# Context sums of six decoded sequences as three products of rounded halves, and four weight tiles loaded later

## The reference

```python
def attend_seq(args):
    pt, qn, qr, cn, krn = args
    c_all = jnp.concatenate([cache_ckv[layer, pt].reshape(past, KV_LORA).astype(cn.dtype), cn], axis=0)
    kr_all = jnp.concatenate([cache_krope[layer, pt].reshape(past, QK_ROPE).astype(krn.dtype), krn], axis=0)
    k_nope = rmsnorm(jnp.einsum('lc,chd->lhd', c_all, w_uk), g_kn)
    s = jnp.einsum('qhd,lhd->hql', qn, k_nope) + jnp.einsum('qhr,lr->hql', qr, kr_all)
    p = jax.nn.softmax(jnp.where(mask[None], s.astype(jnp.float32) * SOFTMAX_SCALE, -jnp.inf), axis=-1)
    ctx = jnp.einsum('hql,lc->qhc', p.astype(c_all.dtype), c_all)
    return jnp.einsum('qhc,chd->qhd', ctx, w_uv).reshape(s_new, N_HEADS * V_HEAD)
```

## Time and profile before

| | |
|---|---|
| median of three runs | 1902.29 us (1901.44 to 1902.49) |
| the profiled execution, its own time | 1903.54 us |
| span in the profile | 1901.7 us |
| TensorE busy | 1872.1 us, 98% of the span |
| VectorE, ScalarE, GpSimd busy | 1098.8, 904.0 and 806.1 us |
| TensorE's granted clock | 0.998 of full speed over the span |

### The profile page before, as it was taken

One profiled execution on the slowest core, in us unless ns is written; L12 is line 12 of the kernel. 1 busy time (PEld: TensorE's weight loads), 2 busy tenths in 40 slices (PEclk: granted clock), 3 DMA queues, 4 the chain that ended last, 5 costly groups with the idle time before them and its releaser, 6 DMA issues.

```text
span 1901.7 us, 35322 instructions
## 1 busy us (share of the span) xinstructions
PE 1872.1 (98%) x13021; PEld 1802.9 (95%) x13021; DVE 1098.8 (58%) x1950; ACT 904.0 (48%) x1858; POOL 806.1 (42%) x814
## 2 busy tenths in 40 slices
PE   7999999999999999999999999999999999999998
PEld 7886679999999999999999999999999999999998
DVE  4677756565556555544645644547773564564464
ACT  4456655554555455343424333347754342433333
POOL 3340013432223224253473474385755347347435
PEclk9999999999999999999999999999999999999999
DMA  5320101211111110222333232232222233323223
GB/s 153 67 57 3 26 20 44 80 33 47 35 39 32 48 35 17 71 80 78 89 89 88 78 98 81 79 109 78 75 79 78 78 88 90 88 83 95 77 86 97
DMA packets 253093, 131.63 MB, mean 69 GB/s; under 512 B 43073, under 2 KB 250754, under 8 KB 252882
## 3 DMA queue, kind: packets, MB, share of 16 engines
q1 hardware_dynamic: 252514, 128.56, 24.2%
q10 hardware_dynamic: 444, 1.29, 0.2%
HBM read 126.21 MB, written 3.61 MB: 68 GB/s over the span
## 4 chain that ended last, share of the span: by engine, by line
PE 94%; DVE 3%; ACT 1%; issue 1%; DMA 1%; SPq 0%; POOL 0%; DVEq 0%; ACTq 0%; POOLq 0%
PE ps L208 13%; PE ps L211 13%; PE ps L209 13%; PE ps L1275 7%; PE ps L1273 7%; PE ps L1274 7%; PE ps L1912 5%; PE ps L1910 5%; PE ps L1916 5%; PE ps L1303 3%; PE ps L259 2%; PE ps L251 2%; PE ps L252 2%; PE ps L1049 2%; PE ps L1240 2%; PE ps L265 1%
## 5 line engine op out<-in xcount | busy, mean ns | idle before, releaser
L208 PE MATMUL ps<-split,whi 128*128 128x288 f32 x1840 | 541.6, 296 | 1.4 <-DVE arena L807 1.0
L209 PE MATMUL ps<-split,whi 128*128 128x288 f32 x1840 | 539.0, 294 | 0.0
L211 PE MATMUL ps<-split,wlo 128*128 128x288 f32 x1840 | 526.7, 295 | 0.0
L195 POOL TENSOR_TENSOR wlo<-raw,whi 128x1024 fp32r<-128x1024 f32 x127 | 307.4, 2423 | 377.7 <-ACT whi L172 370.3
L208 PEld LDWEIGHTS ps<-split,whi 128*128 128x128 f32 x1840 | 345.3, 188 | 3.7 <-issue 3.0
L209 PEld LDWEIGHTS ps<-split,whi 128*128 128x128 f32 x1840 | 345.2, 188 | 0.4
L211 PEld LDWEIGHTS ps<-split,wlo 128*128 128x128 f32 x1840 | 339.9, 188 | 0.0
L1273 PE MATMUL ps<-split,split 128*128 128x384 f32 x768 | 268.2, 349 | 0.0
L1523 DVE TENSOR_REDUCE ssq<-arena 128x16 f32<-128x1024 f32 x128 | 156.1, 1220 | 186.6 <-ACT arena L1385 186.6
L1385 ACT ACTIVATE arena<-ps 128x384 f32<-128x384 f32 (+1 forms) x384 | 174.7, 457 | 184.4 <-PE ps L1275 181.4
L1275 PE MATMUL ps<-split,split 128*128 128x384 f32 x768 | 257.9, 336 | 0.0
(11 more groups left out here) (343 smaller groups left out, 3587.3 us busy)
## 6 DMA issues: line engine op xcount, KB each, us to landing
raw<-in_ffn_w_up SPq DMA_DIRECT2D x96, 512.0 KB, 3.7
raw<-in_ffn_w_down SPq DMA_DIRECT2D x48, 512.0 KB, 3.9
arena<-in_cache_ckv SPq DMA_DIRECT2D x128, 128.0 KB, 2.0
raw<-in_rec_w_in SPq DMA_DIRECT2D x16, 512.0 KB, 3.9
raw<-in_attn_w_o SPq DMA_DIRECT2D x8, 512.0 KB, 5.3
raw<-in_rec_w_out SPq DMA_DIRECT2D x8, 512.0 KB, 4.3
raw<-in_attn_w_down SPq DMA_DIRECT2D x7, 512.0 KB, 7.4
raw<-in_attn_w_uq SPq DMA_DIRECT2D x48, 64.0 KB, 2.1
```

The source lines that it names most:

```text
L195: pool.tensor_tensor(wlo[:, t % RING, :], raw[:, t % RING, :], f32(whi[:, t % RING, :]), ALU.subtract).then_inc(w_lo, 1)
L208: pe.matmul(o, wh, a, start=first, stop=False, skip_group_check=resumed)
L209: pe.matmul(o, wh, b, start=False, stop=False, skip_group_check=resumed)
L211: mm = pe.matmul(o, wl, a, start=False, stop=last, skip_group_check=resumed)
```

## The change

In the tails of sequences 0 to 5 the context sum is made like the other products. ScalarE rounds each cached page (258 columns: the 256, a column of ones and a copy of it) into the memory of `raw`/`wlo` in pages 0 to 7 of the next sequence, two pages of rows in each (`rows_high_act`), GpSimd writes the low halves over the cached rows (`rows_low_pool`), ScalarE rounds the probabilities of part c in page 9+c (`probs_high_act`), VectorE makes their low halves in the same page (`probs_low_dve`), and TensorE multiplies three times for each block (`context_halved`). The tails of sequences 6 and 7 stay as they were. Since `raw` is in use until then, SP loads the four output tiles only in the middle of the last sequence's page loads, when the context of sequence 5 is done. Three smaller edits: the columns of ones are two wide, `cnat` with them, and the last step of the maximum touches the 64 rows that hold new keys.

```diff
-        cnat = sb("cnat", [TN, KL + 1])
+        cnat = sb("cnat", [TN, KL + 2])
...
+        HALVED = NB - 2
+        c_rows = wlo[:].rearrange("p a b -> p (a b)")
+        c_last = area(A_P + 7424, 260, dt=F32R)
+        c_new = sb("c_new", [TN, 264], F32R)
+        c_new_lo = area(A_P + 7424 + 776, KL, dt=F32R)
+        cpg_lo = area(A_QC, 2 * PAGES, 260, dt=F32R)
+        s_lo = [area(A_P + i * SEQ_BLOCKS * HQ, SEQ_BLOCKS, HQ, dt=F32R) for i in range(2)]
+        s_hi_of = [area(A_V + 3328, 5, HQ, dt=F32R), area(A_P + 7424 + 264, 4, HQ, dt=F32R)]
+        row_hi, ROW_HI0 = d_ss, 4
+        row_lo, ROW_LO0 = d_rs, 4
+        prob_hi, PROB_HI0 = d_ln, 3
+        prob_lo, PROB_LO0 = d_sq, 7
+
+        def row_high(k):
+            if k == PAGES:
+                return c_new[:, 0:KL + 2]
+            return c_last[:, 0:KL + 2] if k == PAGES - 1 else c_rows[:, 260 * k:260 * k + KL + 2]
+
+        def row_low(par, k):
+            return c_new_lo[0:TN, :] if k == PAGES else cpg_lo[:, par * PAGES + k, 0:KL]
+
+        def rows_high_act(act, b, par, i):
+
+            if i == 0 and b:
+                act.wait_ge(x_ctx, b)
+            if i == 0 and b == 0:
+                act.copy(row_high(PAGES), cnat[:, :]).then_inc(row_hi, 1)
+            for k in (2 * i, 2 * i + 1):
+                act.copy(row_high(k), cpg[:, par * PAGES + k, 0:KL + 2]).then_inc(row_hi, 1)
+
+        def rows_low_pool(pool, b, par, i):
+
+            if i == 0 and b == 0:
+                pool.wait_ge(row_hi, ROW_HI0)
+                pool.tensor_tensor(row_low(par, PAGES), cnat[:, 0:KL], f32(row_high(PAGES))[:, 0:KL], ALU.subtract)\
+                    .then_inc(row_lo, 1)
+            for k in (2 * i, 2 * i + 1):
+                pool.wait_ge(row_hi, ROW_HI0 + PAGES * b + k + 1)
+                pool.tensor_tensor(row_low(par, k), cpg[:, par * PAGES + k, 0:KL], f32(row_high(k))[:, 0:KL],
+                                   ALU.subtract).then_inc(row_lo, 1)
+            pool.wait_ge(row_lo, ROW_LO0 + PAGES * b + 2 * i + 2)
+
+        def probs_high_act(act, b, par, c):
+            act.wait_ge(x_exp, 4 * b + c + 1)
+            act.copy(s_hi_of[c % 2][:, 0:len(PARTS[c]), :], part(s_all[par], c)).then_inc(prob_hi, 1)
+
+        def probs_low_dve(dve, b, par, c):
+            dve.wait_ge(prob_hi, PROB_HI0 + 4 * b + c + 1)
+            ks = PARTS[c]
+            hi = f32(s_hi_of[c % 2])
+            m = min(ks[-1] + 1, PAGES)
+            ins = dve.tensor_tensor(s_lo[par][:, ks[0]:m, :], s_all[par][:, ks[0]:m, :], hi[:, 0:m - ks[0], :], ALU.subtract)
+            if ks[-1] == PAGES:
+                ins = dve.tensor_tensor(s_lo[par][0:TN, PAGES, :], s_all[par][0:TN, PAGES, :], hi[0:TN, m - ks[0], :],
+                                        ALU.subtract)
+            ins.then_inc(prob_lo, 1)
+
+        def context_halved(pe, b, par, c):
+
+            pe.wait_ge(prob_lo, PROB_LO0 + 4 * b + c + 1)
+            pe.wait_ge(row_lo, ROW_LO0 + PAGES * b + min(PARTS[c][-1] + 1, PAGES))
+            for j, k in enumerate(PARTS[c]):
+                n = P if k < PAGES else TN
+                hi, lo = s_hi_of[c % 2][0:n, j, :], s_lo[par][0:n, k, :]
+                pe.matmul(ps[:, 7, 0:KL + 2], hi, row_high(k), start=(k == 0), stop=False)
+                pe.matmul(ps[:, 7, 0:KL], hi, row_low(par, k), start=False, stop=False)
+                mm = pe.matmul(ps[:, 7, 0:KL + 2], lo, row_high(k), start=False, stop=(k == SEQ_BLOCKS - 1))
+            return mm
...
             if 10 <= i <= 13:
                 if i == 10:
                     pe.wait_ge(x_mbs, b + 1)
-                pe.wait_ge(x_exp, 4 * b + i - 9)
-                for k in PARTS[i - 10]:
+                if b < HALVED:
+                    mm = context_halved(pe, b, par, i - 10)
+                else:
+                    pe.wait_ge(x_exp, 4 * b + i - 9)
+                for k in PARTS[i - 10] if b >= HALVED else ():
                     n = P if k < PAGES else TN
-                    rhs = cpg[:, par * PAGES + k, 0:KL + 1] if k < PAGES else cnat[:, :]
+                    rhs = cpg[:, par * PAGES + k, 0:KL + 1] if k < PAGES else cnat[:, 0:KL + 1]
                     mm = pe.matmul(ps[:, 7, 0:KL + 1], s_all[par][0:n, k, :], rhs, start=(k == 0),
                                    stop=(k == SEQ_BLOCKS - 1))
                 if i == 13:
...
+                if tail and b - 1 < HALVED:
+                    if i < PAGES // 2:
+                        rows_high_act(act, b - 1, 1 - par, i)
+                    if 9 <= i <= 12:
+                        probs_high_act(act, b - 1, 1 - par, i - 9)
...
+                if 1 <= n // PAGES <= HALVED and n % PAGES < PAGES // 2:
+                    pool.wait_ge(kr_in, n + 2)
+                    rows_low_pool(pool, n // PAGES - 1, (n // PAGES - 1) % 2, n % PAGES)
...
-                dve.tensor_tensor(mx, mx, s_all[par][:, PAGES, :], ALU.max).then_inc(x_max, 1)
+                dve.tensor_tensor(mx[0:TN, :], mx[0:TN, :], s_all[par][0:TN, PAGES, :], ALU.max).then_inc(x_max, 1)
...
+                    if b - 1 < HALVED and 9 <= i <= 12:
+                        probs_low_dve(dve, b - 1, 1 - par, i - 9)
...
             wo = proj_src("attn_w_o")
-            sp.wait_ge(p_o, NH)
-            for d in range(4):
-                load_tile(sp, WO0 + d, wo(d))
-            with sp.Fori(0, 3) as r:
+            with sp.Fori(0, 2) as r:
                 for par in range(2):
                     for i in range(PAGES):
                         page_load(sp, r * 2 + 2 + par, par, i, True)
+            for b in (LAST - 1, LAST):
+                for i in range(PAGES):
+                    page_load(sp, b, b % 2, i, True)
+                    if b == LAST and i == 3:
+                        sp.wait_ge(x_ctx, HALVED)
+                        for d in range(4):
+                            load_tile(sp, WO0 + d, wo(d))
             sp.wait_ge(kb_mm, 3 * PAGES * NB)
             sp.dma_start(uv2, I["attn_w_uv"][0].rearrange("(k p) h d -> p k (h d)", p=P)).then_inc(s_uv, 16)
 
```

More of the change, by code:

```diff
@@ L457, in keep_gains @@
             dve.tensor_copy(mask16[:, 1, :], cmask).then_inc(s_gs, 1)
-            dve.memset(cnat[:, KL:KL + 1], 1.0)
+            dve.memset(cnat[:, KL:KL + 2], 1.0)
             dve.wait_ge(s_small, 16 * SMALL_DMAS)
@@ L1160, in prompt_dve @@
                     if u == 32:
-                        dve.memset(cpg[:, 0:PAGES, KL:KL + 1], 1.0).then_inc(s_init, 1)
+                        dve.memset(cpg[:, 0:PAGES, KL:KL + 2], 1.0).then_inc(s_init, 1)
             lo_dve(dve, 0, 0, 0)
@@ L1663, in sample_dve @@
             dve.memset(s_all[1][TN:P, PAGES, :], NEG)
-            dve.memset(cpg[:, PAGES:2 * PAGES, KL:KL + 1], 1.0).then_inc(s_init, 1)
+            dve.memset(cpg[:, PAGES:2 * PAGES, KL:KL + 2], 1.0).then_inc(s_init, 1)
             query_new(dve, 0, 0)
```

## The result

The changed kernel takes 1908.5 us (median of 7 runs, 1908.05 to 1909.06), the kernel before in the same rounds 1902.5 us; the ratio is 1.003, with a 95% interval from 1.002 to 1.004. It is slower by 6.0 us. The forecast was 1906.9 us, slower.

The account below looks back on a forecast made before the run. TensorE's list, busy 98% of the span, was taken as the bound. Per sequence -1.44 + 0.6 + 0.22 + 1.24 = +0.62 us; six give +3.7, with sequence 1's 0.9 +4.6: 1906.9 us, range 1900.5 to 1911.5.

Parts of the forecast that it names:

- The gain: TensorE's context sum: 51 products at 0.120 us replace 34 passes, 6.41 for 7.85 us, saving 1.44 a sequence (0.83 to 1.90).
- Page 10: TensorE waits 1.24 us before the first context product, for VectorE's low halves of part 0 made late in page 9.
- Page 9: Two page copies ahead of ScalarE's query copies in page 7 delay page 9's products by 0.22 us (0 to 0.4).
- Page 3: Low half of page 3 comes late and TensorE waits 0.6 us a sequence, between 0.1 and 1.1.
- the meeting: GpSimd's two further subtractions coincide with VectorE's two maxima; page 3's lateness reaches 1.1 us if each maximum loses.
- the late scaling: GpSimd's scaling, pushed back by its first two subtractions, ends near 583.6, so VectorE loses 0.1 us before page 3.
- The rival in which GpSimd wins both times: Page 3 costs 1.1 us because GpSimd's subtractions hold up both maxima: +3.0 more, 1909.9 us; chance 13%.
- the one in which VectorE does: VectorE wins the ports, so page 3 costs only 0.1 us: 1903.0 us, no change; chance 29%.
- Sequence 1: GpSimd's prompt work stands ahead of its second pair of subtractions, adding 0.9 us to page 3's wait, once.
- Pages 5 to 8: VectorE and GpSimd meet again behind more slack: nothing in the sum, 0.4 us a sequence in the upper bound.
- The tiles: Output tiles loaded in the last sequence cost nothing; if cover were too short, one wait of 3 us at most.
- 1893.7 us: Rival: low halves of part 0 ready in time and VectorE wins in page 3, leaving only the gain; chance 9%.

Follow-up runs that it names:

- the experiment: Against the changed kernel, part 0 of the probabilities is rounded and split in page 8 instead of page 9: 1901.56 us, ratio to the kernel before 0.9995.
- all three moves: Changed kernel with part 0 in page 8, rows of pages 14 and 15 in page 11, GpSimd's pairs behind scaling and maxima: 1897.56 us, ratio 0.9974.
- the kernel with the low halves in the gap: Kernel of all three moves, with VectorE's low halves of part 0 put before page 9's sum of squares, where VectorE waits for ScalarE: 1896.11 us, ratio 0.9961.
- the run with GpSimd's wait: Changed kernel, with GpSimd's two subtractions of page 1 waiting until VectorE's two maxima of that page are done: 1905.98 us, ratio 1.0016.

## Why the prediction was right

**What bounds it.** TensorE's list. Of the +6.0 us, 5.65 are in the six sequences, in the shorter products and in waits of TensorE, as said.

**The gain.** Forecast 1.44 us a sequence at 0.120 us for a product, measured 1.30 (63.75 against the 62.45 of a sequence without a wait). The pace was right: 553.97 to 555.65 are 14 products, 0.120 each. What was left out is the first product of a part, which takes 0.17 without a wait ahead of it (545.39 to 545.56) and 0.20 behind one (553.77 to 553.97), in place of 0.12, four times a sequence. So the four parts without a wait last 1.84, 1.49, 1.48 and 1.76 us, 6.57 in all, where 6.41 was forecast; what they replace was read rightly, 7.87 for 7.85. The formula of the Trainium skill (TensorE: Matmul & The Clock Gate, Back-to-back issue gap) for an isolated product would give 0.110; in this stream the rows have 0.120.

**Page 10.** Forecast 1.24, measured 1.28 by the start of the first product and 1.30 by the distances, since the first product behind the wait also takes longer; the experiment shows its cause: moving the instruction took it away.

**Page 9.** Forecast 0.22, measured 0.21 to 0.23 in the distances, though the start of page 9's products (545.78) shows no idle time; moving the two copies took it away.

**Page 3.** Forecast 0.6, between 0.1 and 1.1, measured 0.56 in sequences 2 to 6. Both parts of the mechanism that was given are there, 0.5 for the meeting and less than 0.1 for the late scaling, but the 0.6 was only the middle between two ends, so that it came this close is in part luck. One meeting took place, not two (instructions of the rows above, one by one):

```profile
587.21 0.75 POOL L1242 TENSOR_TENSOR split<-arena,wlo 128x256 fp32r<-128x256 f32 x1
...
587.31 0.92 DVE L1563 TENSOR_TENSOR arena<-arena 128x256 f32<-128x256 f32 x1
...
588.27 0.42 DVE L1563 TENSOR_TENSOR arena<-arena 128x256 f32<-128x256 f32 x1
```

GpSimd's first subtraction ran beside L1554. Its second started 0.10 us ahead of the first maximum, and this maximum took 0.92 us in place of 0.42 and ended 0.28 after the subtraction; the second maximum met no subtraction. SBUF — State Buffer, in the Trainium skill (section SBUF: two separate sides), has whoever starts first keep the shared ports for its whole instruction; these rows agree. The rival in which GpSimd wins both times, and the one in which VectorE does, both fall.

**Sequence 1.** Forecast 0.9 more in page 3, measured 0.63 there and 0.30 in page 10. That the two add up to the forecast is luck. The forecast had the prompt's work delay the second pair; but that pair cost less than elsewhere (0.39 of the wait went with the meeting, 0.49 in the others), and 0.8 was the scaling, late behind the low half of the new rows (0.74 us) and the pair of page 0. The prediction reckoned with the pair alone and put the scaling's lateness at 0.1. The 0.30 of page 10 was not foreseen: it is VectorE's work of page 9 beside the prompt's work, and it went when page 7's pair was moved.

**Pages 5 to 8** were put at nothing, and in the changed kernel their distances are the old ones. **The tiles** cost nothing.

**The sum.** Forecast per sequence +0.62, measured 64.53 - 63.75 = +0.78; with sequence 1 +4.6 against +5.65 in the trace. In each of six sequences the gain was 0.14 too large and page 10 0.06 too small, against 0.04 too much in page 3. The rest up to +6.0 lies within what the medians can tell. Two of the rivals' sums leave terms out, without effect on the forecast: 1893.7 us holds neither the 0.22 of page 9 nor the 0.1 of page 3, 1.9 us over six sequences, and 1903.0 us not the 0.9 of sequence 1.

## What to carry to other kernels

Where one engine is always busy, shorter instructions on it are worth only what the helpers' new work leaves, and that is decided in single pages: not by a helper's busy share (GpSimd went from 28% to 49% of a sequence without being a bound) but by what stands directly ahead of the one instruction that is waited for. Put a new helper instruction behind the instruction that the busy engine waits for next, at a place where the helper itself waits; here the same work at other places turned +6 us into -7. Moving work moves the later meetings of VectorE and GpSimd too (page 9 to 10 with all three moves, page 10 to 11 of sequence 1 without page 7's pair), so the timeline has to be read again after each move. And the first sequence with the new work is worth its own reading: work that is done only once stood there ahead of what was waited for.

## What the runs showed of the hardware that was not expected

The first of a row of fp32r products that follows the rope product costs 0.17 us even without a wait (545.39 to 545.56 in the kernel with the low halves in the gap), the next ones 0.12. And the cost of a meeting between VectorE and GpSimd falls on both. In the changed kernel a subtraction of GpSimd takes 1.21 us where VectorE started 0.06 ahead of it, in place of 0.73, and a VectorE instruction on 64 x 128 elements takes 0.70 beside GpSimd's subtraction (590.06 to 590.95), in place of 0.29 in the run with GpSimd's wait:

```profile
543.70 0.68 DVE L1581 TENSOR_TENSOR arena<-arena 128x512 f32<-128x512 f32 x1
543.76 1.21 POOL L1242 TENSOR_TENSOR split<-arena,wlo 128x256 fp32r<-128x256 f32 x1 [1.16 <-ACT wlo L1232]
...
590.39 0.70 DVE L1571 TENSOR_TENSOR arena<-arena 64x128 f32<-64x128 f32 x1
```
